# The relative-position bias tables read by 17 transfers of 7 or 8 partitions, with 8 copies of each line in DRAM

## What is computed

```python
dist = ATTN_BLOCK + qi - si                     # 128 queries, 256 keys
bias = rel_bias_table.astype(jnp.float32)[t5_bucket(jnp.maximum(dist, 0))]   # 32 buckets, 16 heads
scores = jnp.where(valid, scores + bias, NEG_INF)
...
def head_bias(dist):                            # second block, 8 heads
    return jnp.transpose(rel_table[rel_bucket(dist)], (2, 0, 1)).reshape(G, R, *dist.shape)
...
def block_fn(args):                             # the experts: what most of the time goes to
    xb, eb, gb = args
    a = jnp.einsum('cd,ced->ce', xb, u_tab[eb]).astype(jnp.float32)
    w = (gb * jax.nn.gelu(a, approximate=False)).astype(xb.dtype)
    return jnp.einsum('ce,ced->cd', w, v_tab[eb])
```

## Time and profile before

| what | value |
|---|---|
| median of 3 runs | 3290.94 us (3282.7 to 3293.37) |
| profiled execution, its own time | 3282.93 us |
| its span | 3281.1 us |
| TensorE busy | 2445.8 us, 75% |
| VectorE busy | 2320.1 us, 71% |
| ScalarE busy | 1330.7 us, 41% |
| DMA | 1295.01 MB, 395 GB/s over the span |
| granted TensorE clock, mean | 0.85 |

### The profile page before, as it was taken

The page is one execution under the profiler, slowest core; times in us unless marked ns, Lnnn a source line. Parts: engine busy times, 40 slices in busy tenths (PEclk is TensorE's granted clock), DMA queues, the critical chain, the costliest instruction groups (busy, mean ns, idle before and its releaser), DMA issues.

```text
span 3281.1 us, 40578 instructions
## 1 busy us (share of the span) xinstructions
PE 2445.8 (75%) x14052; PEld 1029.2 (31%) x14052; DVE 2320.1 (71%) x5500; ACT 1330.7 (41%) x3602; POOL 1129.2 (34%) x1038
## 2 busy tenths in 40 slices
PE   8868779776797777979787869878887655554555
PEld 3442333223332233335342426423334211111111
DVE  7439694778839787385875685987866777777644
ACT  2114432444424444243583343467734433333322
POOL 0012342324413243243343333443433444443432
PEclk9979889987898988989888979878888877778777
DMA  9899999999999999999999999999999999999997
GB/s 247 304 351 415 399 410 386 411 397 414 413 389 416 415 411 412 371 397 401 383 379 388 397 402 399 406 419 410 378 411 400 413 420 420 419 418 409 420 420 318
DMA packets 214057, 1295.01 MB, mean 395 GB/s; under 512 B 26934, under 2 KB 30294, under 8 KB 82776
## 3 DMA queue, kind: packets, MB, share of 16 engines
q0 software_dynamic: 148320, 1076.50, 80.9%
q1 hardware_dynamic: 64860, 213.81, 17.2%
q10 hardware_dynamic: 672, 2.12, 0.2%
HBM read 1289.62 MB, written 2.71 MB: 394 GB/s over the span
## 4 chain that ended last, share of the span: by engine, by line
PE 35%; DMA 25%; DVE 22%; issue 8%; ACT 4%; POOL 3%; SPq 0%; POOLq 0%; DVEq 0%; ACTq 0%
PE ps L1722 12%; DMA ring<-in_k_uv,idx 10%; DMA ring<-in_k_vu,idx 9%; PE ps L1802 9%; DVE ring L415 9%; DMA wsl<-in_k_wu 6%; PE ps L2096 6%; POOL ring L2400 3%; DVE big L470 2%; PE ps L2106 2%; ACT L1249 2%; PE ps L1779 1%; PE ps L1977 1%; DMA wsl<-in_k_wmod 1%; ACT diag L1249 1%
## 5 line engine op out<-in xcount | busy, mean ns | idle before, releaser
L1722 PE MATMUL ps<-ring,diag 64*64 64x512 f32 x8192 | 1255.7, 738 | 483.1 <-ACT diag L1249 459.1
L415 DVE CUSTOM_DVE_ANT_0 ring<-ring,xn 128x1024 f32<-128x1024 f32 x1024 | 1238.8, 1220 | 440.9 <-DMA ring<-in_k_vu,idx 231.7
L2400 POOL DMA_INDIRECT ring<-in_k_vu,idx x514 | 559.5, 1089 | 1136.7 <-DVE aw L415 645.6
L2400 POOL DMA_INDIRECT ring<-in_k_uv,idx x510 | 563.6, 1105 | 940.1 <-DVE aw L415 643.2
L1722 PEld LDWEIGHTS ps<-ring,diag 64*64 64x64 f32 x8192 | 308.2, 157 | 1240.0 <-ACT diag L1249 733.2
L1249 ACT ACTIVATE aw<-aw 128x2 f32<-128x2 f32 x512 | 103.7, 202 | 1008.8 <-DVE aw L415 1007.3
L1802 PE MATMUL ps<-wsl,xT 128*128 128x512 f32 x896 | 427.6, 623 | 36.5 <-DMA wsl<-in_k_wu 32.3
L1249 ACT ACT_TABLE_LOAD x339 | 434.9, 1283 | 22.8 <-issue 10.7
L1249 ACT ACTIVATE diag<-gid,aw 128x64 f32<-128x64 f32 x1024 | 312.0, 342 | 315.1 <-PE ps L1722 298.9
L1249 ACT ACTIVATE gid<-ident,gate 128x64 f32<-128x64 f32 x1024 | 292.4, 332 | 0.0
L1802 PEld LDWEIGHTS ps<-wsl,xT 128*128 128x128 f32 x896 | 167.0, 196 | 296.0 <-issue 226.4
(11 more groups left out here) (264 smaller groups left out, 2112.1 us busy)
## 6 DMA issues: line engine op xcount, KB each, us to landing
wsl<-in_k_wu SPq DMA_DIRECT2D x342, 512.0 KB, 8.8
wsl<-in_k_wmod SPq DMA_DIRECT2D x40, 512.0 KB, 6.4
ring<-in_k_vu,idx POOLq DMA_INDIRECT x514
ring<-in_k_uv,idx POOLq DMA_INDIRECT x510
ring<-in_k_wmod SPq DMA_DIRECT2D x8, 512.0 KB, 10.5
wsl<-in_k_wu SPq DMA_DIRECT2D x8, 280.0 KB, 26.4
hres<-in_x SPq DMA_DIRECT2D x4, 512.0 KB, 6.0
pers<-L1d POOLq DMA_DIRECT2D x8, 256.0 KB, 13.0
```

Of the source, the lines that this page charges most:

```text
L415: V(v.tensor_tensor_reduce(u_row(s), u_row(s), xn[:, n % 3, :], 1.0, 0.0, ALU.mult, ALU.add, aw[:, b, k:k + 1]), ("dot", s))
L1722: r = t.matmul(PA[half][64 * q:64 * q + 64, :], diag[64 * half:64 * half + 64, s % (2 * PAIR), :], v_row(s)[64 * half:64 * half + 64, 512 ...
L2400: Q(p.indirect_dma_start(out=both_rows(s), out_offset=None, in_=tab, in_offset=bass.IndirectOffsetOnAxis(ap=idx[:, n % 2, k:k + 1], axis=0 ...
```

## The change

`L1d` and `L2d` keep 8 copies of a head's line rather than 16, and the copies are no longer shifted: all begin at element 0 of their row. One transfer now fills the partitions i, i + 17, i + 34 and so on up to 127, that is 8 partitions for i from 0 to 8 and 7 for i from 9 to 16. Its m-th partition reads copy m; the step of one row less 17 elements gives it the right shift. Seventeen such transfers fill a table where there were eight. The bytes written into SBUF stay the same, 2 MB for `bias1` and 1 MB for `bias2`; the bytes stored in DRAM are halved, from 384 to 192 KB and from 192 to 96 KB.

```diff
-        L1d = nc.dram_tensor("L1d", [16, 16, WC], F32, kind="Internal").ap()
-        L2d = nc.dram_tensor("L2d", [8, 16, WC], F32, kind="Internal").ap()
+        L1d = nc.dram_tensor("L1d", [16, 8, WC], F32, kind="Internal").ap()
+        L2d = nc.dram_tensor("L2d", [8, 8, WC], F32, kind="Internal").ap()
...
-        def shifted(copies, heads, a):
-
-            return bass.AP(tensor=copies.tensor, offset=128 - 16 * a, ap=[[WC, 16], [16 * WC, heads], [1, 256]])
+        def shifted(copies, heads, i):
+
+            return bass.AP(tensor=copies.tensor, offset=127 - i, ap=[[WC - 17, 8 - i // 9], [8 * WC, heads], [1, 256]])
 
         def copied(copies, heads):
 
-            return bass.AP(tensor=copies.tensor, offset=1, ap=[[16 * WC, heads], [WC + 1, 16], [1, W1]])
+            return bass.AP(tensor=copies.tensor, offset=0, ap=[[8 * WC, heads], [WC, 8], [1, W1]])
...
-            Q(p.dma_start(copied(L1d, 16), bc(lv.unsqueeze(1), [16, 16, W1])), "bias_d0", ("bias_d", 0))
+            Q(p.dma_start(copied(L1d, 16), bc(lv.unsqueeze(1), [16, 8, W1])), "bias_d0", ("bias_d", 0))
...
-            for a in range(8):
-                Q(p.dma_start(bias1[16 * a:16 * a + 16, :, :], shifted(L1d, 16, a)), "bias0",
-                  *([("bias", 0)] if a == 7 else []))
+            for i in range(17):
+                Q(p.dma_start(bias1[i::17, :, :], shifted(L1d, 16, i)), "bias0",
+                  *([("bias", 0)] if i == 16 else []))
...
-                    for a in range(8):
-                        Q(s.dma_start(bias2[16 * a:16 * a + 16, :, :], shifted(L2d, 8, a)), "bias1",
-                          *([("bias", 1)] if a == 7 else []))
+                    for i in range(17):
+                        Q(s.dma_start(bias2[i::17, :, :], shifted(L2d, 8, i)), "bias1",
+                          *([("bias", 1)] if i == 16 else []))
```

More of the change, by code:

```diff
@@ L2378, in gpsimd_program @@
             lv = BB[0]["lv"][0:16, 0:W1]
-            Q(p.dma_start(copied(L1d, 16), bc(lv.unsqueeze(1), [16, 16, W1])), "bias_d0", ("bias_d", 0))
+            Q(p.dma_start(copied(L1d, 16), bc(lv.unsqueeze(1), [16, 8, W1])), "bias_d0", ("bias_d", 0))
             G.wait_ge("bias_lv", 1)
             lv = BB[1]["lv"][0:8, 0:W1]
-            Q(p.dma_start(copied(L2d, 8), bc(lv.unsqueeze(1), [8, 16, W1])), "bias_d1", ("bias_d", 1))
+            Q(p.dma_start(copied(L2d, 8), bc(lv.unsqueeze(1), [8, 8, W1])), "bias_d1", ("bias_d", 1))
             G.wait_ge("bias_d", 0)
             G.wait_ge("win", 0, 3)
-            for a in range(8):
-                Q(p.dma_start(bias1[16 * a:16 * a + 16, :, :], shifted(L1d, 16, a)), "bias0",
-                  *([("bias", 0)] if a == 7 else []))
+            for i in range(17):
+                Q(p.dma_start(bias1[i::17, :, :], shifted(L1d, 16, i)), "bias0",
+                  *([("bias", 0)] if i == 16 else []))
             G.wait_ge("s_y", 0, 3)
```

## The result

The changed kernel is slower by a little: 3287.77 us (median of 20 runs) against 3284.36 us for the kernel before (20 runs). These medians lie 3.4 us apart. The ratio is estimated from the single runs and not from the two medians; it is 1.0021 with a 95% interval of 1.0011 to 1.0031, or +6.9 us (+3.6 to +10.2). One of the 20 runs before took 3809.45 us, a slow one, and is not in the ratio. The profiled execution has a span of 3286.4 us against 3281.1. The forecast was +1.5 us, no difference that a measurement can tell. The sign and the place were right. The size was not, and neither of the two terms that it was added up from came true.

What follows compares the result with a forecast made beforehand. Gathers and weights fill the DMA engines; elsewhere TensorE's fixed order sets the pace, in the opening TensorE and VectorE. 0 + 0 + 0 + 3.6 - 2.07 = +1.5 us on 3290.94 gave 3292.4 us, range 3281 to 3303.

Steps and rivals of the forecast that it cites:

- The stores: Stores of the table lines into DRAM shrink by half, and nothing on the chain waits for them: 0 us.
- GpSimd's issue: Nine more issues of bias1 on GpSimd, at most 5.1 us more, ahead of the gather at 217.13 us: 0 us.
- the table's first use: VectorE reads bias2 at 1615.06 us, 127 us after its last landing, so no delay of the table counts: 0 us.
- The landing of the first table: bias1 lands near 62 to 75.7 us, before VectorE reads it at 77.75: 0 us, bounds -0.8 and 0.
- rival D: At bias1, each transfer has its own price, 2.8 us, whatever its bytes; VectorE waits, about +19 us; chance 0.04.
- The issue of the second table: Seventeen bias2 issues on SyncE take 8.8 us, delaying the weight unit behind: +3.6 us, bounds 0 and +5.8.
- The relief: At bias2, slow traffic from 16 neighbouring partitions written at once goes away: -2.07 us, bounds -2.07 and 0.
- Rival B: bias2 occupies half of the DMA engines, so the weight unit behind lands 11.8 us later; chance 0.17.
- B's milder form: At bias2, gathers dry out during the wait, leaving SyncE's queue the engines, and traffic speeds up: +2 to +6 us.
- C: The weight unit behind bias2 lands before TensorE needs it; wait and slow first matmuls go: -6.6 us; chance 0.17.
- forecast A: Whole kernel: the main forecast, effect behind 1455 us at the second table, +1.5 us, range 3288 to 3297; chance 0.62.
- The last sign: Up to the second table, the first 1455 us differ by no more than 2 us, else the forecast's reason is wrong.

Runs made afterwards that it cites:

- e5: Kernel before, but both tables by 8 transfers of 16 partitions 8 apart, from 16 unshifted copies: ratio 0.9999 (0.9986 to 1.0013).
- e7: Kernel before, but both tables in 16 partitions 8 apart and the second's transfers spread over 8 later weight units: 0.9967 (0.9955 to 0.9978), median 3271.04 us.
- e6: Kernel before, but the second table's 8 transfers issued one ahead of each of 8 later weight units: 0.9980 (0.9967 to 0.9993), median 3276.65 us.
- e2: Kernel before with only the second table changed to 17 transfers, 17 apart, from 8 unshifted copies: ratio 1.0043 (1.0030 to 1.0055).
- e3: Kernel before, but the second table read by 16 transfers of 8 neighbouring partitions from the shifted copies: ratio 1.0040 (1.0025 to 1.0055).
- e8: Changed kernel, but the second table's 17 transfers spread ahead of 8 later weight units: ratio to the kernel before 1.0007 (0.9994 to 1.0021).
- e10: Kernel before plus, after its last output, four forms alone, 32 KB a partition, from SyncE then GpSimd; SyncE's moved 52, 95, 97 and 155 GB/s.
- e9: Kernel before plus, after its last output, the second table's shapes alone; from SyncE 16 neighbours 9.4 us, 17 apart 15.0, 8 apart 7.5.
- e4: Kernel before, but each of the second table's 8 transfers cut in two by heads, 16 partitions each: ratio 1.0007 (0.9996 to 1.0018).

## Why the prediction was partly right

- **The stores, GpSimd's issue, the table's first use: 0 us.** They stand. Seventeen issues on GpSimd took 10.08 us; I had 9.6, from 0.566 each, and they take 0.601.
- **The landing of the first table: 0 us, "VectorE doesn't notice".** The step failed, its effect didn't. I let the table land between 62 and 75.7 us since its bytes are the same. It landed near 80.4, and VectorE waited 3.43 us for it. What I had left out is that the last of 17 issues is 5.1 us later and the relief that should have made up for it didn't come. The half time that the prediction put beside it wasn't seen either: from the first issue to the last landing it took 31.5 us (48.9 to 80.4), and 26.3 before. That the late table cost nothing on the path is due to the 4.00 us of idle time behind, which I had noted under rival D only.
- **The issue of the second table: +3.6 us.** This is the step that failed most: I took the time of an issue as fixed, and SyncE can be held in it. I multiplied a median issue of 0.475 us by 17 and got 8.8 us; it was 30.4. The single issue of 1.48 us in the earlier trace rows was the sign of it: SyncE was already being held there. In the kernel before run again the 8 issues took 12.66 us, in its first profile 5.16, and I had only the smaller.
- **The relief: -2.07 us.** It didn't come. The wider spacing does speed up the writes (the forms alone), but the engines it needs were halved at the same time, and in e5, where they weren't, the time stayed the same. Only with the transfers spread as well (e7 beside e6) did the wider spacing go with a shorter time, by 5.6 us in the medians.
- **Rival B, +11.8 us, chance 0.17.** Its premise is what the forms alone show, half of the engines, and its effects came: a wait of 14.95 us (I had 17), gathers that stop for 18.91 us. Its path was another. I had let the weights lie longer behind the table; in fact SyncE issued them 30.4 us after the table's first transfer, and they landed 12.79 us after that. Its sign that the last transfer takes over 30 us to land can't be read, since the trace has no landing time for these transfers. I priced it by the wait, while TensorE's time of going on moved by 5.5 us and the ratio says +6.9, just above B's milder form, +2 to +6. That form was the nearest forecast for the whole change. For the second table alone (e2, +14 us) even the full price is too low, and why the two differ stays open.
- **C and D.** C's wait that goes was seen only where the transfers were moved. D's release by a DMA was seen, but the price of 2.8 us a transfer was not: 17 transfers landed within 27 us, 1.7 us each. That is above the 1.35 us from which I had said that D decides, and its effect stayed in VectorE's idle time.
- **The signs.** By them forecast A's reason was wrong. Of its five only the traffic held (180 GB/s where 150 went). The first table was to land before 72 us and did near 80.4; VectorE was to start at 77.7 to 77.8 us, released by TensorE, and did at 80.55, released by a DMA; the unit was to be issued near 1468 us and was at 1484.26; the wait was to be 3 to 10 us and was 14.95. That the time still lay close to the forecast is luck: +3.6 and -2.07 were both wrong. The weights were issued 30.4 us after the table's first transfer rather than 5.16, and only the 5.5 us by which TensorE went on later are seen in the time. The last sign, that the first 1455 us differ by no more than 2 us, was too strict to tell: SyncE's first issue of the second table came 5.3 us earlier in the changed kernel, and in the kernel before run again 2.7 us earlier than in its first profile.

## What to carry to other kernels

A transfer of 8 or 7 partitions from SyncE took 8 or 7 DMA engines here and one of 16 took all, so count partitions before you spread them: alone, 16 partitions spaced wide (155 GB/s) beat both 16 neighbours (97) and 8 partitions spaced wider (95). Look at what stands behind a burst of transfers in the same queue; moving the burst behind the weights that are needed next was worth 0.2% (e6), where no shape of the burst in its old place gained anything. A bad shape cost more than that, 0.4% in e2 and e3, and the better place didn't take that away (e8 stands 0.4% above e7, with the first table's form in it too). And price a wait by when the waiting engine goes on, in more than one execution, not by how long it waited.

## What the runs showed of the hardware

- Writes to SBUF have a rate that goes with the spread of the partitions. In the middle of its stretch, 8 neighbours moved 49 to 55 GB/s in most slices, 16 neighbours 97 to 104 and 16 partitions 8 apart 182 to 194 (e10, each stretch in 40 equal slices, in this order):

```profile
GB/s 0 10 26 79 144 63 49 49 55 51 53 53 96 67 53 55 51 51 51 49 65 89 67 53 59 49 51 51 55 83 85 61 51 51 53 31 14 8 2 0
```

```profile
GB/s 0 34 62 240 184 104 97 98 100 99 100 119 144 106 104 98 100 100 99 100 133 138 106 100 97 102 100 99 100 138 134 104 100 102 98 85 42 8 0 0
```

```profile
GB/s 0 0 0 0 82 79 157 309 351 227 188 182 194 188 194 185 188 185 188 182 188 185 194 182 188 182 191 194 176 197 188 203 188 185 182 178 94 33 0 0
```

  The Trainium skill's map (SBUF — State Buffer, section on the DMA port swizzle) gives them 2, 4 and 8 ports, and 27.2 GB/s for each. By that map the slices come to 23 to 28 GB/s for each port in all three (an estimate), which agrees.
- A DMA's share near 1 says that the engines hold packets, not that they move data: 1.01 stood with 97 GB/s.
- From GpSimd the 17-apart form made 560 packets under 512 B where 8 transfers of 16 partitions made 128 (e9). What the others are isn't shown. Four 8-partition transfers from GpSimd had a share of 0.74, which is more than eight engines gave from SyncE (0.41 and 0.49, e10).
- SyncE can be held within an issue while the gathers run: up to 4.40 us in the changed kernel and 8.60 in e8, with 8 engines. With 16 it also happens (up to 4.49 us in e4). With nothing else under way the same 17 issues took 0.68 to 0.85 us each (e9). That the queue of the engines that it feeds is full then is a reading that fits; no run shows a queue's length.
